# A two-layer transformer kernel: pooled branch and second attention with float32 products

## The reference, cut to what matters

```python
cs = jnp.cumsum(ug, axis=1)                                # pooled branch
outs.append((c - lagged) / count - ug[:, :, g])
mixed = jnp.einsum('bsgc,gcd->bsgd', pooled, pool_w)
b = mixed.reshape(B, S, WIDTH_B) * pool_scale * jax.nn.silu(z_b)
...
probs = jax.nn.softmax(jnp.concatenate([scores, sink], axis=-1), axis=-1)[..., :-1]
out = jnp.einsum('bnkgqj,bnjkd->bnqkgd', probs, vb)        # second attention
```

## Time and profile before

| | |
|---|---|
| median of three runs | 3410.5 us (3409.02 to 3413.55) |
| profiled execution, its own time | 3413.96 us |
| its span, first to last instruction | 3412.2 us |
| TensorE busy, share of the span | 3171.1 us, 93% |
| VectorE / ScalarE / GpSimd busy | 1775.7 / 1563.3 / 999.2 us |
| mean granted TensorE clock | 0.950 of full |

### The profile page before, as it was taken

How to read it: one execution, slowest core, us unless ns; L and a number is a source line. 1 busy time by engine, 2 the same in 40 slices (tenths; PEclk the granted TensorE clock), 3 DMA queues, 4 the chain that set the end, 5 groups by cost and what they waited for, 6 DMA issues and landing times. The chain is left out here.

```text
span 3412.2 us, 43258 instructions
## 1 busy us (share of the span) xinstructions
PE 3171.1 (93%) x15878; PEld 2617.5 (77%) x15878; DVE 1775.7 (52%) x3672; ACT 1563.3 (46%) x2454; POOL 999.2 (29%) x742
## 2 busy tenths in 40 slices
PE   7995999889996999978999979978999999989998
PEld 7994888667875777756887858867888888868787
DVE  6775799888995665524441156651312132233433
ACT  4444689756983777721111033333544354431111
POOL 3540012100231766621222133322322232222222
PEclk9996999889997999976999989989999999989999
DMA  6666333443334211046553245537434644445522
GB/s 180 194 194 219 92 94 99 124 154 89 99 90 162 70 41 51 26 157 243 154 150 108 93 171 168 161 116 233 131 124 143 224 130 133 131 138 155 146 99 87
DMA packets 434156, 458.18 MB, mean 134 GB/s; under 512 B 30896, under 2 KB 318128, under 8 KB 432304
## 3 DMA queue, kind: packets, MB, share of 16 engines
q1 hardware_dynamic: 433968, 455.72, 42.7%
HBM read 289.70 MB, written 165.94 MB: 134 GB/s over the span
## 5 line engine op out<-in xcount | busy, mean ns | idle before, releaser
L1312 PE MATMUL p_pr<-p_hT,p_w_hi 128*128 128x512 f32 x896 | 356.3, 398 | 13.0 <-POOL p_w_lo L1095 9.6
L2453 PE MATMUL p_pr<-p_hT,p_w_hi 128*128 128x512 f32 x896 | 352.0, 393 | 15.0 <-DMA p_hT<-s_hT 15.0
L1313 PE MATMUL p_pr<-p_hT,p_w_hi 128*128 128x512 f32 x896 | 354.1, 395 | 0.0
L1314 PE MATMUL p_pr<-p_hT,p_w_lo 128*128 128x512 f32 x896 | 353.9, 395 | 0.0
L2454 PE MATMUL p_pr<-p_hT,p_w_hi 128*128 128x512 f32 x896 | 350.7, 391 | 0.0
L2455 PE MATMUL p_pr<-p_hT,p_w_lo 128*128 128x512 f32 x896 | 350.0, 391 | 0.0
L1518 POOL TENSOR_TENSOR a_prob<-a_prob,a_inv 128x1024 f32<-128x1024 f32 (+12 forms) x104 | 250.5, 2419 | 188.6 <-DVE a_inv L1563 188.4
L1095 POOL TENSOR_TENSOR p_w_lo<-p_w_raw,p_w_hi 128x256 fp32r<-128x256 f32 x144 | 108.0, 781 | 619.4 <-DVE p_level L1232 401.6
L1135 ACT ACTIVATE p_relu<-p_isc,p_level 128x2048 int8<-128x2048 f32 (+5 forms) x192 | 276.5, 1442 | 21.8 <-DVE p_level L1232 17.6
L808 PE MATMUL t_pj_ps<-t_w_hi,t_hT_slot 128*128 128x356 f32 (+2 forms) x768 | 270.9, 353 | 11.8 <-DVE t_w_lo L662 5.6
L810 PE MATMUL t_pj_ps<-t_w_hi,t_hT_slot 128*128 128x356 f32 (+2 forms) x768 | 264.1, 344 | 0.0
(11 more groups left out here) (277 smaller groups left out, 7063.7 us busy)
## 6 DMA issues: line engine op xcount, KB each, us to landing
p_w_raw<-in_w_in SPq DMA_DIRECT2D x112, 512.0 KB, 4.3
s_hT<-t_hT_slot SPq DMA_DIRECT2D x32, 1024.0 KB, 6.0
p_hT<-s_hT SPq DMA_DIRECT2D x64, 512.0 KB, 9.8
s_gT<-p_o_sb SPq DMA_DIRECT2D x128, 256.0 KB, 4.8
o_gates<-s_gT SPq DMA_DIRECT2D x64, 512.0 KB, 5.1
s_qT<-t_qT_slot SPq DMA_DIRECT2D x32, 512.0 KB, 2.7
s_zuT<-p_o_sb SPq DMA_DIRECT2D x64, 256.0 KB, 4.8
pl_wada<-in_w_ada SPq DMA_DIRECT2D x6, 2048.0 KB, 13.6
```

Of the source, the lines that this page charges most:

```text
L1312: nc.tensor.matmul(pr[n % NPR][:], wh, hi, start=(k == 0), stop=False)
L1313: nc.tensor.matmul(pr[n % NPR][:], wh, lo, start=False, stop=False)
L1314: last = nc.tensor.matmul(pr[n % NPR][:], wl, hi, start=False, stop=(k == KD - 1))
L2453: nc.tensor.matmul(pr[n % NPR][:], wh, hi, start=(k == 0), stop=False)
```

## The change

Three parts. In `phase_pool` every input has its own buffer (four `u`, four `z`, five of `w_ada`), and SP issues the loads without a wait for a group's end; the stores come last. The splits are gone, the map is one float32 product per 512 columns, all six chunks of `w_ada` are done as eight products of 512 columns giving a row repeated on all partitions, and VectorE takes the columns out of the first four rows with 16 small multiply-and-sum instructions against the identity. The order on TensorE is: map 0, chunk 0, map 1, chunk 1, map 2, chunk 2, chunk 3, map 3, chunk 4, chunk 5. In `phase_tokens` the second block's values are stored once and unsplit. In `phase_second` the weighing is done as in the first attention, by two float32 products in column tiles per key tile; `pt` has four slots, and the low part and its VectorE instruction are gone.

```diff
 phase_tokens
-    v = sb("v_slot", [P, 2, 2, NKV, 2, HD], F32R) if second else sb("v_slot", [P, 2, NKV, HD], F32)
+    v = sb("v_slot", [P, 2, NKV, HD], F32)
-                for g in range(NKV if second else 0):
-                    nc.gpsimd.tensor_tensor(v[:, slot, 1, g], vsrc[:, g], f32(v[:, slot, 0, g]), ALU.subtract)
-                    last = nc.scalar.activation(v[:, slot, 0], spread(values, 2, 2), ACT.Copy)
+                last = nc.scalar.activation(v[:, slot], values, ACT.Copy)
 phase_pool, SP
+            load_u(0)
+                sp.dma_start(w[:], ...); c_col; bada; gpre
+            load_ada(0); load_u(1); load_z(0); load_ada(1); load_u(2); load_z(1)
+            load_ada(2); load_u(3); load_z(2); load_z(3)
+            for n in range(3, N_ADA):
+                load_ada(n)                     # n = 5 waits for rowed >= 1
+            for g in range(G):
+                sp.wait_ge(out_done, g + 1)
+                sp.dma_start(c.bT[g], z[:, g]).then_inc(stored, 16)
+                if g == 1:                      # gate_b, g_post into u[:, 0]
 phase_pool, ACT: only the sigmoid; GpSimd: only the memset
 phase_pool, DVE
+                if g:
+                    dve.wait_ge(mapped, g)      # before pooled[:] is written
+            def columns(n):
+                dve.wait_ge(rowed, n + 1)
+                for j in range(4):
+                    nc.vector.tensor_tensor_reduce(out=unread[:], in0=row[n % 4][:, j * P:(j + 1) * P], in1=c.ident[:], ...
+            for g in range(G):
+                pool_group(g)
+                if g == 0:
+                    c_act = c_col * c_sig
+                else:
+                    finish(g - 1)
+                    columns(g - 1)
+            finish(G - 1)
+            columns(G - 1)
 phase_pool, PE
+            def ada(n):
+                for k in range(KD):
+                    last = nc.tensor.matmul(row[n % 4][:], c_act[:, k:k + 1].to_broadcast([P, P]), wada[:, n % NW, k, :], ...
+            def pool_map(g):
+                pe.wait_ge(pooled_done, g + 1)
+                if g:
+                    pe.wait_ge(out_done, g)
+                for j in range(GROUPS):
+                    last = nc.tensor.matmul(m_ps[:, cols], w[:, g], pooled[:, cols], start=True, stop=True)
 phase_second
-    NT = 2
+    NT = 4
-                    nc.tensor.matmul(o_ps[:], vh, pt[:, n % NT, 0], start=(j == 0), stop=False)
-                    nc.tensor.matmul(o_ps[:], vh, pt[:, n % NT, 1], start=False, stop=False)
-                    nc.tensor.matmul(o_ps[:], vl, pt[:, n % NT, 0], start=False, ...).then_inc(weighed, 1)
+                    for half, p in ((0, slice(0, HD)), (1, slice(HD, P))):
+                        last = nc.tensor.matmul(o_ps[p], v[:, i % 2, at, g, :], pt[:, n % NT, half::2, :], ...)
-                    nc.vector.tensor_tensor(pt[:, n % NT, 1], ...)      # low_parts
-                for half, p in ((0, slice(0, HD)), (1, slice(HD, P))):
-                    nc.vector.tensor_tensor(aT[p, s], o[p, half::2, :], z[p, s], ALU.mult).then_inc(gated, 1)
+                nc.vector.tensor_tensor(aT[:, s]..., o_ps[:], z[:, s]..., ALU.mult).then_inc(gated, 1)
```

More of the change, by code:

```diff
@@ L203, in constants @@
     return load_gcol, load_positions, load_rows, rows_waited, squares, band, sines, frequencies, angles, rows, wait_ident, wait_gcol
[L206 to L271, removed]
@@ L1669, in phase_pool @@
     G = len(WINDOWS)
-    u = sb("u", [P, 2, HALO + SEQ], F32)
-    z = sb("z", [P, 2, SEQ], F32)
+    N_ADA = 3 * D // BANK
+    NW = 5
+    u = sb("u", [P, G, HALO + SEQ], F32)
+    z = sb("z", [P, G, SEQ], F32)
     run = sb("run", [P, 2, HALO + SEQ], F32)
[L1673 to L1679, removed]
-    m_ps = ps("m_ps", [P, SEQ])
[L1681 to L1686, removed]
+    pooled = sb("pooled", [P, SEQ], F32)
+    w = sb("w", [P, G, P], F32)
+    wada = sb("wada", [P, NW, KD, BANK], F32)
+    c_col = sb("c_col", [P, KD], F32)
+    c_sig = sb("c_sig", [P, KD], F32)
+    c_act = sb("c_act", [P, KD], F32)
+    bada = sb("bada", [P, 2 * KD], F32)
+    col = sb("col", [P, 2 * KD], F32)
+    unread = sb("unread", [P, P], BF16)
+    gpre = sb("gpre", [P, KD], F32)
+    m_ps = ps("m_ps", [P, SEQ])
+    row = [ps(f"row{n}", [P, BANK]) for n in range(4)]
+    c_loaded, w_loaded, halo = sem("c_loaded"), sem("w_loaded"), sem("halo")
+    u_loaded, z_loaded = [sem(f"u_loaded{g}") for g in range(G)], [sem(f"z_loaded{g}") for g in range(G)]
+    ada_loaded = [sem(f"ada_loaded{n}") for n in range(N_ADA)]
+    sig_done, c_ready, rowed, taken = sem("sig_done"), sem("c_ready"), sem("rowed"), sem("taken")
+    chain, pooled_done, mapped, out_done, stored = (sem("chain"), sem("pooled_done"), sem("mapped"), sem("out_done"),
+                                                    sem("stored"))
+    GATE = 4
     with nc.Block() as block:
@@ L1703, in _, with load_ada @@
[L1703 to L1708, removed]
+            def load_ada(n):
+                if n >= NW:
+                    sp.wait_ge(rowed, n - NW + 1)
+                sp.dma_start(wada[:, n % NW], c.w_ada_2[0, :, n * BANK:(n + 1) * BANK].rearrange("(k p) n -> p k n", p=P)
+                             ).then_inc(ada_loaded[n], 16)
@@ L1710, in _ @@
+            sp.wait_ge(stored, 16 * G)
         @block.gpsimd
@@ L1712, in _ @@
             nc.gpsimd.memset(u[:, :, 0:HALO], 0.0).then_inc(halo, 1)
[L1713 to L1717, removed]
         @block.scalar
         def _(act):
-            ada_sigmoid(act)
-            act.wait_ge(w_loaded, 16)
-            nc.scalar.activation(w_hi[:], w_raw[:], ACT.Copy).then_inc(w_hi_done, 1)
[L1724 to L1727, removed]
-                nc.scalar.activation(p_hi[:, g % 2], pooled[:, g % 2], ACT.Copy).then_inc(hi_done, 1)
+            act.wait_ge(c_loaded, 16 * 3)
+            nc.scalar.activation(c_sig[:], c_col[:], ACT.Sigmoid).then_inc(sig_done, 1)
         @block.vector
@@ new lines, in _ @@
+            dve.wait_ge(taken, 4 * GATE)
+            step(nc.vector.tensor_tensor(bada[:], bada[:], col[:], ALU.add))
+            nc.vector.tensor_copy(c.ada_b[:], bada[:, 0:KD])
+            nc.vector.scalar_tensor_tensor(out=c.ada_a[:], in0=bada[:, KD:2 * KD], scalar=1.0, in1=gpre[:], op0=ALU.add, op1=ALU.mult)
+            dve.wait_ge(rowed, N_ADA)
+            dve.wait_ge(c_loaded, 16 * 5)
+            for n in range(2):
+                part = slice(n * BANK, (n + 1) * BANK)
+                last = nc.vector.tensor_tensor(gate_b[:, part], row[(GATE + n) % 4][:], gate_b[:, part], ALU.add)
@@ L1770, in _ @@
+            step(last)
+            nc.vector.tensor_tensor(c.gpost_gate[:], g_post, gate_b, ALU.mult)
         @block.tensor
         def _(pe):
-            pe.wait_ge(w_lo_done, 1)
-            for g in range(G):
-                s = g % 2
-                ada_product(pe, g)
-                pe.wait_ge(lo_done, g + 1)
+            def ada(n):
+                pe.wait_ge(ada_loaded[n], 16)
+                if n >= 4:
+                    pe.wait_ge(taken, 4 * (n - 3))
+                for k in range(KD):
+                    last = nc.tensor.matmul(row[n % 4][:], c_act[:, k:k + 1].to_broadcast([P, P]), wada[:, n % NW, k, :],
+                                            start=(k == 0), stop=(k == KD - 1))
+                last.then_inc(rowed, 1)
@@ L2358, in _ @@
                 if turn is not None:
-                    high_parts(turn)
+                    copy_keys(turn)
                 turn = turn_at(n, SCORES_AT)
@@ L2426, in _ @@
             for n in range(N_UNITS):
-                turn = turn_at(n, KEYS_AT)
-                if turn is not None:
-                    low_parts(turn)
                 turn = turn_at(n, SCORES_AT)
```

139 lines of the change are left out of this document (71 added, 68 removed).

## The result

The changed kernel took 3371.38 us, the median of four runs (3370.03 to 3373.09), against 3410.16 (3409.02 to 3413.55) for the kernel before on the same chip: a ratio of 0.9885 (95% interval 0.9873 to 0.9897), 38.8 us faster. Brackets behind a ratio are this interval from here on. The prediction was 3389, with a range down to 3375.

A forecast was written before the change was run, and what follows sets the result against it. TensorE was taken as full in the second attention, the pool phase as a chain of waits. Pool phase -34, second token phase -4.5 and second attention +17 gave -21.5 us from 3410.5: 3389 us, range 3375 to 3404.

The forecast's parts named there:

- Pool phase: Pool phase: loads without waits, no splits and dense float32 products take 34 us off, bounds 30 and 38.
- allowed 2 us: Pool phase start: time allowed for loading the parameters in 4-byte pieces ahead of chunk 0; no row showed it.
- The clock charge of 1.5 us for a gap: Pool phase: TensorE's wait before map 2 may drop its clock, costing about 2.5 us; 1.5 was charged.
- the 3 us before map 2: Pool phase: TensorE waits 3 us for VectorE's chunk 0 columns, group 2 additions and product with z.
- The rival of loads not all in flight: Pool phase: SP's queue or the engines pass 270 GB/s instead of 403, giving 3403 us in all; chance 8%.
- that of a low clock: Pool phase: TensorE stays at 1.2 GHz throughout, the phase ends 12.7 us later, 3436 us in all; chance 5%.
- Float32 maps need twice the array time: Pool phase: said of the new maps as the reason the change leans on TensorE's clock.
- Second token phase: Last two tiles: TensorE's wait for GpSimd shrinks as the values' low part goes; -4.5 us, bounds -3.7 and -6.5.
- The 1.9 us per tail: Last two token tiles: the values' low part, 1.82 us, and 0.1 for a shorter ScalarE copy go; 3.8 in all.
- The hope of 0.7 us more: End of the second token phase: a shorter wait may keep TensorE's clock up, worth up to 2.5 us more.
- term of +17: Second attention: float32 halves cost more than three fp32r products per key tile; 17 us slower, bounds +13 and +21.
- The rival of the overlap: Second attention: column tiles run concurrently, 0.47 against 0.71 us per key tile, -15 instead of +17, 3357 in all; chance 5%.

The follow-up runs named there:

- pool_only: The kernel before with only the changed kernel's pool phase put in; 3376.41 us, ratio 0.9902 to the kernel before.
- gps_after: The changed kernel with VectorE's low parts of the second token phase held until GpSimd has made the keys' low part; 3369.15 us, a single execution.
- one_group: The changed kernel with both halves of the weighing written to one column group, leaving out upper heads' attention and the key-tile sum; 3392.95 us, ratio 0.9955.
- early: The changed kernel with group 1's `u` loaded before chunk 0, two parameter vectors moved later and another map and chunk order on TensorE; 3369.69 us, ratio 0.9874.
- early2: The changed kernel with group 1's `u` early, another TensorE order, and two parameter vectors issued behind all loads; 3368.45 us, ratio 0.9885.
- serial_loads: The changed kernel with the pool phase's loads in the old order, group g's waiting until group g-2 is finished; 3399.70 us, ratio 0.9971.

## Why the prediction was wrong, step by step

**Pool phase: right.** Predicted -34, measured -35.0.

- The first addition of VectorE starts 5.08 us after the first issue (predicted 5.1); map 0 starts 10.25 after it, and chunk 0 starts 6.4 after that, where 6.0 were predicted.
- Chunks take 7.0 us each, maps 3.5 at full clock, as predicted. The wait before map 1 is 3.23 us, against 2.0.
- The longer gap comes from the parameters. They were allowed 2 us, "and it would have to be over 4 to be felt"; SP stood 5.3 us on the three of them (1482.44 to 1487.78), and `u` of group 1 landed 17.05 us into the phase instead of 15.3. It was felt at map 1, not at chunk 0.
- The clock charge of 1.5 us for a gap was 3.1, and came at map 1 instead of map 2: the clock is 0.91 in the gap and 0.53 after it. For this the 3 us before map 2 did not come: VectorE was about as late as forecast, but TensorE, with the longer gap and the slow map, reached map 2 at 1521.9, when z's product was done. What was put down as wait and clock at map 2 was paid at map 1. That the sum stayed within 1.0 us is in part luck: 1.2 us more of gap and 1.6 more of clock stand against 3.0 of a wait that didn't come.
- The loads: 339 GB/s in the mean and about 400 while they ran. SP did stand on its queue, 17.7 us on the last three chunks together, but nothing behind it was wanted. The rival of loads not all in flight is out, and so is that of a low clock.
- Two slips weigh little. "Float32 maps need twice the array time" doesn't follow from its rows: 7.0 us at half clock against 5.26 is 1.33 times. And 1557.9 with 0.6 twice and 1.22 is 1560.3, not 1560.6.

**Second token phase: right in what goes, wrong in what takes its place.** The term was -4.5; measured -0.2. The 1.9 us per tail presumed that the keys' pair stays at its 0.86 once the values' pair goes. It took 1.82, so that 0.93 was left per tail, 1.9 in all. The trace of before hid even that: it has the products behind the second tail at full clock (the first at 2296.42 takes 0.33), where after has them at half (0.47, and 0.41 for each that follows), worth 1.2 us. That is no work of the change: `pool_only`, with the token phase of before, has them at half as well, and its phase is 329.38 us; `gps_after` has them at full clock. Against `pool_only`, after's 327.44 is the 1.9. The hope of 0.7 us more, that a shorter wait keeps the clock up, was wrong: the transposes behind 3.86 us took the same 1.94 as behind 4.79.

**Second attention: the step that failed.** It is the sentence "a key tile is eight records there, and sixteen run from 1472.39 to 1474.27, 1.88 us ... So a pair of key tiles costs 1.88" and its term of +17. A key tile is four records, so those sixteen are four key tiles, and the eight in 1.02 us are two. The same rows then give 0.43 to 0.51 per key tile, against 0.71. The count could have been had from the trace of before: L1649 has 1088 records there, and the copies of ScalarE before them (L1603) 272, one per key tile. From this error came the next: "The trace of the first attention does not agree" with the rule of the Trainium skill, "TensorE: Matmul & The Clock Gate", "Part 3: Packing small matmuls". It does agree: the single records of the earlier trace rows start in pairs, 0.01 us apart, with 0.22 from pair to pair. And `one_group` shows it in the new kernel by taking the overlap away: 1.87 for eight records in one column group, 1.01 in two. So the term of +17 is a gain, -3.8 in this pair of traces and -4.3 in the mean of all.

The rival of the overlap, given 5%, named the right mechanism and had a wrong price, -15. It took 0.47 for each key tile and left out the edge of a block. By the rows of after, 30 pairs win 1.41 less 1.20, and 2 turns with one key tile lose 0.77 less 0.71: -6.2 us, where the phase gained 4.3 in the mean. So most of what the overlap brings, 62 x 0.40 = 25 us against the same products in one group, goes to pay for float32 in place of fp32r (0.86 against 0.71 per key tile, 9 us) and for the 11 us at the edges. The last 2 us stay open.

**The sum.** The error of 17.6 us is 20.8 from the second attention and 1.0 from the pool phase, less 4.3 from the token phase. The range took its width from the bounds of each term as read, and no bound allowed for a wrong count.

## What to carry to other kernels

Before a price per product is taken from grouped records, count them: divide a line's count in the whole trace by the number of times its loop runs, and check it against a line of another engine in the same loop. Before a small load or a helper's work is moved, ask who is beside it in the new place; a saving on an engine that shares its time with another can come out as half. Ask of every DMA that is moved what stands behind it in the queue: in `early` it was a load, in `early2` the stores. Where loads wait in the chain, put them in flight first: here 27 of 35 us hung on it.

## What the runs showed of the hardware that was not expected

- Float32 products of 64 output partitions in two column groups overlap fully: 0.43 us per pair of 256-column products, as against 0.86 in one group. Each block of them, in one group or in two, has some 0.34 us at its edges, which float32 products of 128 partitions among the same fp32r products don't have.
- A gap of 3.23 us before TensorE's work was followed by a map at half clock (6.74 us), one of 2.11 us by a map at full clock (3.67). The gap of 2.55 us in `serial_loads` was also followed by full clock. The gap alone doesn't settle it: in the last tail of the token phase the same code, behind the same gap of 4.79 us and transposes at half clock, went on at full clock in before (0.33 us for the next product) and at half in `pool_only` (0.47).
- DMAs of 4 to 8 KB in 4-byte pieces held SP for 0.5 to 3.8 us with at most one large load issued before them, and for 3.7 to 12.3 us with five or more (`early`, `early2`). A load of 1 MB held it up to 7.98 us in after and 10.42 in `early2`, so a few KB in such pieces can stand for as long as a megabyte.
- GpSimd's and VectorE's subtractions side by side: GpSimd's took 0.96 and 0.90 us in place of 0.46 and 0.45, VectorE's second 0.94 in place of 0.68. They take turns rather than share.
